# A streaming encoder layer on one NeuronCore: TensorE's instruction stream for both feed-forward blocks, written out straight in place of a loop

## The reference

```python
def half_ffn(x, g, w_up, w_down):
    a, b = jnp.split(rmsnorm(x, g) @ w_up, 2, axis=-1)
    return x + 0.5 * ((jax.nn.silu(a) * b) @ w_down)

# x <- half_ffn(x, ...)                     first feed-forward block
# x <- x + W_out(gated sum of sparse attention and mLSTM of rmsnorm(x))
# x <- half_ffn(x, ...)                     second feed-forward block
# y = rmsnorm(x)
```

## Time and profile before

| what | value |
|---|---|
| runs shown | 2861.8, 2865.97, 2872.58 us; median 2865.97 |
| profiled execution: span from the first to the last instruction | 2870.8 us |
| PE busy | 2711.6 us (94%), 15459 matmul records |
| DVE / ACT / POOL busy | 1198.2 / 700.1 / 725.5 us |
| DMA queue of data | 152.45 MB, 17.9% of the engines' time |
| instruction fetches | queue q8: 128 packets, 2.10 MB; queue q14: 33 packets, 0.27 MB |
| mean granted TensorE clock | 0.962 |

### The profile page before, as it was taken

The page is one execution under the profiler, slowest core; times in us unless marked ns, Lnnn a source line. Parts: engine busy times, 40 slices in busy tenths (PEclk is TensorE's granted clock), DMA queues, the critical chain, the costliest instruction groups (busy, mean ns, idle before and its releaser), DMA issues. The chain is left out here.

```text
span 2870.8 us, 39037 instructions
## 1 busy us (share of the span) xinstructions
PE 2711.6 (94%) x15459; PEld 2619.8 (91%) x15459; DVE 1198.2 (42%) x2109; ACT 700.1 (24%) x1258; POOL 725.5 (25%) x396
## 2 busy tenths in 40 slices
PE   7999999999998899999876898998999999999998
PEld 6999999999997599999864686998999999999998
DVE  5121222222234699999544795423222222212126
ACT  5111111111114311211163774212311111111112
POOL 5322222222214012111221311422422222222221
PEclk8999999999999999999966899999999999999999
DMA  4111111111103111132222201431111111111101
GB/s 136 34 45 45 45 44 32 44 45 45 45 1 125 39 46 44 55 93 84 86 45 51 45 1 56 140 114 52 45 45 45 36 39 45 45 45 40 35 30 74
DMA packets 193661, 154.81 MB, mean 54 GB/s; under 512 B 32292, under 2 KB 178128, under 8 KB 193244
## 3 DMA queue, kind: packets, MB, share of 16 engines
q1 hardware_dynamic: 193500, 152.45, 17.9%
HBM read 124.56 MB, written 23.90 MB: 52 GB/s over the span
## 5 line engine op out<-in xcount | busy, mean ns | idle before, releaser
L356 PE MATMUL f1ps_up<-xn_lo,f1w_hi 128*128 128x384 f32 x1056 | 356.6, 338 | 18.5 <-issue 9.7
L356 PE MATMUL f2ps_up<-xn_lo,f2w_hi 128*128 128x384 f32 x1056 | 356.5, 338 | 16.7 <-issue 10.5
L357 PE MATMUL f2ps_up<-xn_hi,f2w_lo 128*128 128x384 f32 x1056 | 355.4, 337 | 0.0
L357 PE MATMUL f1ps_up<-xn_hi,f1w_lo 128*128 128x384 f32 x1056 | 355.3, 336 | 0.0
L358 PE MATMUL f2ps_up<-xn_hi,f2w_hi 128*128 128x384 f32 x1056 | 355.1, 336 | 0.0
L358 PE MATMUL f1ps_up<-xn_hi,f1w_hi 128*128 128x384 f32 x1056 | 355.0, 336 | 0.0
L356 PE MATMUL d_ps<-xn_lo,d_w_hi 128*128 128x384 f32 x888 | 302.0, 340 | 7.0 <-POOL xn_lo L311 5.5
L357 PE MATMUL d_ps<-xn_hi,d_w_lo 128*128 128x384 f32 x888 | 300.7, 339 | 0.0
L358 PE MATMUL d_ps<-xn_hi,d_w_hi 128*128 128x384 f32 x888 | 300.6, 339 | 0.0
L508 DVE TENSOR_TENSOR f2hid<-f2gate,f2ps_up 128x384 f32<-128x384 f32 x66 | 36.6, 554 | 519.1 <-ACT f2gate L477 519.1
L508 DVE TENSOR_TENSOR f1hid<-f1gate,f1ps_up 128x384 f32<-128x384 f32 x66 | 36.6, 554 | 518.4 <-ACT f1gate L477 518.4
(11 more groups left out here) (302 smaller groups left out, 5397.7 us busy)
## 6 DMA issues: line engine op xcount, KB each, us to landing
f1raw<-in_w_ffn_up SPq DMA_DIRECT2D x44, 512.0 KB
f2raw<-in_w_ffn_up SPq DMA_DIRECT2D x44, 512.0 KB
d_raw<-in_w_in SPq DMA_DIRECT2D x37, 512.0 KB, 4.1
p_dram<-stage SPq DMA_DIRECT2D x21, 576.0 KB, 3.1
f1raw<-in_w_ffn_down SPq DMA_DIRECT2D x11, 1024.0 KB
f2raw<-in_w_ffn_down SPq DMA_DIRECT2D x11, 1024.0 KB
b_sg<-p_dram SPq DMA_DIRECT2D x16, 576.0 KB, 4.9
x_dram<-xT SPq DMA_DIRECT2D x1, 4608.0 KB, 15.0
```

Source lines behind the costliest of these rows:

```text
L356: nc.tensor.matmul(out, w_hi, x_lo, start=first, stop=False)
L357: nc.tensor.matmul(out, w_lo, x_hi, start=False, stop=False)
```

## The change

PE's call of `run` gets no loop object, and `run` then repeats the passes in Python: the five passes of both blocks are written out one after the other in PE's program, and the waits compare with constants. ACT, POOL, DVE and SP keep their loops. The other two users of loops are untouched.

```diff
@@ run
-            with loop(0, BODIES) as i:
-                for n0 in range(2, 8):
-                    before(i, n0 + 1)
-                    pair(i, n0, *PAIRS[n0])
+            if loop is None:
+                for i in range(BODIES):
+                    for n0 in range(2, 8):
+                        before(i, n0 + 1)
+                        pair(i, n0, *PAIRS[n0])
+            else:
+                with loop(0, BODIES) as i:
+                    for n0 in range(2, 8):
+                        before(i, n0 + 1)
+                        pair(i, n0, *PAIRS[n0])
             pair(BODIES - 1, 8, *LAST)
@@ block.tensor
-                run(nc.tensor.Fori, lambda i, n0: None, pair)
+                run(None, lambda i, n0: None, pair)
```

## The result

The change took the kernel from 2867.66 us (median of 4 runs, 2861.8 to 2872.58) to 2833.75 us (2833.4 to 2838.83). The ratio is 0.9876 with a 95% interval of 0.9854 to 0.9899, so it is faster by 1.0 to 1.5%. In a second comparison, beside other kernels, the same kernel had 2833.59 us against 2867.06 (ratio 0.9889, 0.9859 to 0.9919).

The account below looks back on a forecast made before the run. PE, busy for 94% of the span, was taken to bound the kernel. Pauses and slow passes, 2.7 + 3.0 + 22.0 + 3.5 = 31.2 us, come off 2866.0, giving 2835 us, range 2828 to 2850.

Parts of the forecast that it names:

- the narrow range: The likeliest case's own range for the whole kernel's time: 2829 to 2841 us around 2835.
- The branch and not a late product: At pass ends in both blocks: PE's pause comes from its back branch, not from another engine's late result.
- (a): At the back branches of both blocks: eight PE pauses leave, 2.68 us at the first block's first, 3.03 in the second.
- (b): Passes after the pauses: 22.0 us too long in passes 2 to 4, 3.5 in the last passes, partly TensorE's clock.
- only the pauses leave: Rival for both blocks: the clock still falls now and then without pauses, so 2845 us; chance 0.11.
- The pace of 0.32 us: Behind the first pause, where the clock is 0.50: time per matmul, against 0.1733 us without a pause.
- (c): PE's loop: register steps and branches, some 67 rows a pass, leave and waits get constants; worth nothing.
- (d): PE's passes 2 to 5: new addresses add no fetches, about 12 of 128 packets fewer; price 0.
- The rate of one per 20 us: PE's program queue in straight code and first pass: ten packets from 33 to 234 us, taken as block crossings.
- (e): After a pass end: ACT's and POOL's splits, loads and DVE still come in time, with 18 us to spare for splits.
- The fetch as the cause: At PE's back branches over a long body: the target is fetched again, about one to two packets each.
- the other reading: TensorE's memory holds 2048 instructions, so a pass of 1728 stays on the core; gain near 0.

Follow-up runs that it names:

- e2_others: Kernel before, with ACT, POOL, DVE and SP written out straight in both blocks and TensorE keeping its loops: 2867.86 us, ratio 1.0005.
- e4_wait: Kernel after, with TensorE waiting for ScalarE's rounding of the next unit's weights at the start of passes 2 to 5 of both blocks: 2868.57 us, ratio 1.0011.
- e3_hint: Kernel before, TensorE's loop kept in both blocks, with a hint on its closing branch (hint_back_edge=True): 2840.18 us.
- e6_eight: Kernel after, but TensorE's second projection loop goes twice round eight units instead of eight times round two: 2837.4 us.
- e9_ten: Kernel after, but TensorE's projection loops are replaced by one going twice round ten units: 2836.17 us.
- e5_tiny: Kernel after, with TensorE going four times round a tiny loop of one satisfied wait at the start of passes 2 to 5 of both blocks: 2852.15 us.
- e1_first: Kernel before, with only the first block's passes written out straight on TensorE, the second block keeping its loop: 2852.4 us, ratio 0.9947.

## Why the prediction was right

The median came out at 2833.75 against 2835 forecast, inside the narrow range. The level is closer than the gain was: the gain came out at 33.9 and not 31.2, and the kernel before had 2867.66 beside it and not 2865.97. Step by step:

- *The branch and not a late product.* Right. Straight code on the other engines changed nothing (e2_others); with TensorE's loop gone, no wait inside the blocks is left.
- *(a) and (b), 31.2 us.* The blocks gave 30.7 in the traces. The two parts were pauses, 21.5 us, and clock, about 10; e4_wait gave them back at 18.4 + 10.5 without a branch. The forecast from the second pass's first matmul to the end of the first block was 623.9 us; it is 859.13 - 235.29 = 623.84. The rival "only the pauses leave" (2845) is out: the clock was 1.00 in all windows of the blocks shown above. (The pace of 0.32 us that the prediction cites for the low clock is not in the earlier trace rows; 3.41 / 11 = 0.31 from the earlier trace rows is.)
- *(c) Register steps and branches at nothing.* Right: they run at full pace in e3_hint.
- *(d) Fetches at nothing.* Right for the time: over 70 crossings into new code without a pause. The count was off: 109 packets where 112 to 118 were forecast. The rate of one per 20 us was misread: the tenth packet of the earlier trace rows, at 230.1, is the read-ahead past the loop's end and no crossing, and the kernel after has nine in the same 33 to 234 us. Over both blocks it is 76 packets, one per 22 us, and a back branch had brought 19 / 8 = 2.4 too many and not 1.5.
- *(e) Nobody late next.* Right: ACT's split behind the first pass now starts at 235.57 and POOL's at 237.56, as long after PE's last down matmul as before, and nothing waited for them:

```profile
235.57 1.92 ACT L431 ACTIVATE f1w_hi<-f1raw 128x2048 fp32r<-128x2048 f32 x1 [21.59 <-PE f1ps_dn L358]
237.56 4.60 POOL L435 TENSOR_TENSOR f1w_lo<-f1raw,f1w_hi 128x2048 fp32r<-128x2048 f32 x1 [18.90 <-ACT f1w_hi L431]
```

- *The fetch as the cause.* Right, but the reason given against the other reading was not. The prediction dismissed a memory of 2048 instructions because nine packets came in each repeated pass. With the hint none comes, so a pass does fit; 5.8 blocks are kept without any hint, 7 are mostly not (2 of 28 back branches in the blocks), 14 are not even with it. The Trainium skill, "Runtime: NRT & Kernel Launch", section Instruction fetch mechanics, states 128 KiB for TensorE, and that agrees with e3_hint. It also states that a branch outside the two-block window stalls; e6_eight and e9_ten disagree, with back branches over 4.6 and 5.8 blocks at 0.17 us from start to start. What fits all runs is that the sequencer, reading on past the end of the body, lays new blocks over the head of the loop, so that seven blocks and the look-ahead don't both fit into eight; the hint keeps it from reading on. The packets show that in the blocks a read-ahead went before every lost pass, and that there was none with the hint or where the pass was kept. That it is laid over the loop's head is argued from this, not shown by itself.

The measured gain of the medians, 33.9 and 33.5 us, is a little over the 31.2; its intervals include that. What a single profiled pair of spans shows beyond it (8.7 us) is the spread of single executions.

## What to carry to other kernels

When the bounding engine shows an idle time that no semaphore explains at a loop's end, look at its program queue in the DMA view: packets in every round mean that the body isn't kept. Count the body in packets of program: here one held some 250 matmuls and weight loads (19008 of them in the two straight blocks came with 76 packets). Keep it under six packets, hint the back branch at seven, or write it straight; the price of straight code was nothing here, 76 packets without a pause. Where "issue" or another engine's name stands at the pause, compare it with the packet's time and with the waits in the program: both labels were wrong or empty here. Count the clock with the pause: in e4_wait a stall of 2.3 us of TensorE cost 3.6 on the mean. And before believing a difference of a few microseconds in a stage that wasn't touched, profile the old kernel a second time.

## What the runs showed that was not expected

The projection runs at one of three paces, by execution and not by kernel. Windows of the same 170 us, with the count of matmuls in brackets behind PE's busy time, of the kernel before, e5_tiny, e1_first and the kernel after:

```profile
1210.00:1380.00 170.00, 170.00 (x964) 170.00 (x964) 162.20 (x328) 32.09 (x53) 31.25 (x13) 1.00 0.30 91
```

```profile
1210.00:1380.00 170.00, 170.00 (x965) 170.00 (x963) 162.11 (x332) 32.02 (x53) 31.30 (x13) 1.00 0.28 88
```

```profile
1210.00:1380.00 170.00, 170.00 (x975) 170.00 (x974) 162.07 (x336) 33.41 (x55) 33.60 (x14) 1.00 0.28 87
```

```profile
1210.00:1380.00 170.00, 170.00 (x983) 170.00 (x982) 162.07 (x336) 33.01 (x56) 33.68 (x14) 1.00 0.28 86
```

A matmul that only reaches into the window counts too, so the pace is 170.34 / 964 = 0.1767 us, and for the others 0.1765, 0.1747 and 0.1733, at the full granted clock; from start to start e5_tiny has 0.1767 as well. The kernel before had 0.1767 in one profile and 0.1733 in the other, the hinted loop 0.1733 and 0.1747. Over the stage's 2664 matmuls of this kind the outer two paces differ by an estimated 9 us; the stage took 531.4 to 542.2 us in the fourteen profiles. The first block ran at 0.1733 in all of them, away from its pauses. What sets the pace is open.
